# One 512 column matmul for the high and low parts of the activations, in a hybrid Conformer and gated linear attention trunk

## The chip, the cores and the metric

The kernel runs on one core of one Trainium2 chip. Its metric is the device time of one execution in microseconds. One more execution was taken by the hardware profiler: every row below comes from that one. TensorE (PE in the profile) multiplies matrices into the accumulation memory PSUM, which has 8 banks of 512 float32 columns in each of 128 partitions. VectorE is DVE, ScalarE is ACT, GpSimd is POOL, and SyncE (SP) issues the loads.

## The reference

Two layers work on 256 tokens of width 2048, in float32. Layer 0 mixes tokens with a causal Conformer convolution module, layer 1 with chunked gated linear attention (GLA). Each mixer is followed by a SwiGLU network of inner width 5632, and each half has an RMS norm ahead of it:

```
h = rms_norm(x, norm_mix_g[i]);  x = x + mixer(h)
a, g = split(rms_norm(x, norm_ffn_g[i]) @ w_gate_up[i])
x = x + (silu(a) * g) @ w_down[i]
```

At the end stands a last RMS norm. What matters here is the dense products: activations of 256 tokens by weights of 2048 (or 5632) rows.

## The kernel before

Activations lie transposed: 128 channels of one tile on the partitions, 256 tokens (T) along the columns; 16 tiles make the width of 2048. A weight matrix comes from memory in chunks of 128 x 4 x 512 float32 (1 MB), four row tiles by 512 output channels, into a ring of four buffers (`raw`). For each chunk ScalarE writes the high part `w_hi` (a copy into the type fp32r, L435), and VectorE or GpSimd writes `w_lo = raw - w_hi` (L673, L337). The activations are split in the same way, `x_hi` and `x_lo` for the normed input of a block, `h_hi` and `h_lo` for the hidden values. These four were separate SBUF tensors of 16 KB in each partition, `x_lo` right behind `x_hi`, `h_lo` right behind `h_hi`.

A product of a chunk (`chunk`, L1067) is three fp32r matmuls of 256 columns for each of its 4 x 4 pairs of row tile and output block of 128 channels, all accumulated in the same 256 columns: `w_hi` by the high part, `w_hi` by the low part, `w_lo` by the high part. Every matmul loads its 128 x 128 weights anew. A group is the chunks (4, or 3 in the last part of a SwiGLU network) that sum up 512 output channels. Two accumulators of two banks each, `slot[0]` and `slot[1]`, take groups in turn; the semaphore `acc_read[s]` says that slot s has been read and may be used again (`free_slot`). PE counts each chunk that it has done in `w_used`; the ScalarE copy of chunk c waits for chunk c - 4 in it, so the splitting runs three chunks ahead (`AHEAD`).

The dense stages, in the order in which PE runs them: the convolution's input product (`conv_product`, L1138, other tiles); its output product (`residual_product`, 16 chunks); SwiGLU of layer 0 (132 chunks); q and k (16 chunks, `group`), v (16 chunks, L1299, 512 columns, where the activations are the stationary operand and the weights move); levels of the attention; the GLA gate (16 chunks, `group`); the GLA output product (16 chunks); SwiGLU of layer 1 (132 chunks); the transposed output rows.

A SwiGLU network runs in three parts of 4, 4 and 3 pairs. In one pair, slot 0 takes the 512 channels of `a` (half 0), slot 1 those of `g` (half 1). VectorE multiplies slot 0 by the norm's factor `rstd` (L883), ScalarE takes Silu (L578), VectorE multiplies by `rstd` again (L887) and by slot 1 (L891); ScalarE writes `h_hi` (L581), VectorE `h_lo` (L894). Then four groups of the down product add to the residual stream `res` (L850, with a bias L854), which ScalarE squares for the next norm (L463) and scales into `x_hi` (L468), and VectorE sums up (L695, L698) and splits (L726). The sum over partitions for the norm is a matmul with ones into `stat` (`statistic`, L1086), issued between half 0 and half 1 of the first pair; ScalarE takes its root (L450).

All engines work through their instructions in the order of the program, each with its own stream of waits. PSUM is full: slot 0 and slot 1 in two banks each, `stat`, `pair_s0`, `pair_s1` and `misc` in one each.

## Time and profile before

| | |
|---|---|
| median of 3 runs | 2326.99 us (2325.85 to 2328.06) |
| profiled execution, its time | 2326.2 us |
| its span, first to last instruction | 2324.4 us |
| mean granted TensorE clock | 0.991 of full speed |
| PE busy | 2283.1 us, 98% |
| DVE, ACT, POOL busy | 1318.9 us, 953.7 us, 274.5 us |
| read from memory | 396.91 MB, 172 GB/s over the span |

Matmuls are pipelined. The duration of one (283 ns for 256 columns) runs over the start of the next; what a matmul costs is the distance from start to start, which the timeline shows, or the length of an unbroken stretch divided by its count.

### The profile page before, as it was taken

To read this page: it belongs to the slowest core of one execution; us is meant where nothing else is said; L and a number is where in the kernel's file an instruction comes from. 1 tells how busy PE (TensorE), PEld (TensorE's weight loads), DVE (VectorE), ACT (ScalarE), POOL (GpSimd) and SP (SyncE) were. 2 spreads that over 40 slices of the span, in tenths; PEclk is the share of its full clock that TensorE was granted. 3 is DMA by queue.
4 is the path that set the end of the run, shared out by engine and by line. 5 is a ranking of instruction groups with operands and counts; after the bars stand their busy time and mean duration, and the time that the engine had idled before them with its cause. 6 is when DMAs were issued, how large, how long until landed. Compare 5 with 4: busy or idle time off the path is not lost.

```text
span 2324.4 us, 43601 instructions
## 1 busy us (share of the span) xinstructions
PE 2283.1 (98%) x18476; PEld 2255.2 (97%) x18476; DVE 1318.9 (57%) x1204; ACT 953.7 (41%) x822; POOL 274.5 (12%) x126
## 2 busy tenths in 40 slices
PE   7999899999999999999999999999999999999998
PEld 6999799999999999999998799999999999999998
DVE  6999756545444544445666656665454445444554
ACT  6555544333333333334444344444333333333443
POOL 4988200000000000000006610000000000000000
PEclk9999899999999999999999999999999999999999
DMA  7655255555555555555454335555545555555541
GB/s 205 184 160 164 90 185 188 187 182 181 181 181 180 181 182 188 176 192 184 162 170 142 130 109 187 176 192 175 195 172 190 181 182 182 182 186 185 184 166 73
DMA packets 249951, 400.48 MB, mean 172 GB/s; under 512 B 6375, under 2 KB 72111, under 8 KB 249823
## 3 DMA queue, kind: packets, MB, share of 16 engines
q1 hardware_dynamic: 249406, 398.74, 51.1%
q8 instruction: 79, 1.29, 0.2%
q0 software_dynamic: 240, 0.23, 0.1%
q14 instruction: 18, 0.15, 0.0%
q10 hardware_dynamic: 208, 0.07, 0.0%
HBM read 396.91 MB, written 2.10 MB: 172 GB/s over the span
## 4 chain that ended last, share of the span: by engine, by line
PE 87%; issue 5%; DVE 4%; POOL 2%; ACT 1%; DMA 1%; SPq 0%; POOLq 0%; DVEq 0%; ACTq 0%
PE slot L1067 81%; DVE dec L965 1%; POOL w_lo L337 1%; PE pair_s L1284 1%; PE slot L1299 1%; PE slot L1138 1%; DMA raw<-in_conv_w_in 1%; ACT dec L620 0%; DVE dec L964 0%; PE pair_s L1127 0%; POOL y_sum L381 0%; DVE dec L971 0%; DVE dec L972 0%; PE misc L1192 0%; PE misc L1239 0%
## 5 line engine op out<-in xcount | busy, mean ns | idle before, releaser
L673 DVE TENSOR_TENSOR w_lo<-raw,w_hi 128x2048 fp32r<-128x2048 f32 x327 | 746.8, 2291 | 742.1 <-ACT w_hi L435 742.1
L435 ACT ACTIVATE w_hi<-raw 128x2048 fp32r<-128x2048 f32 x376 | 717.0, 1910 | 820.2 <-PE slot L1067 803.0
L1067 PE MATMUL slot<-x_hi,w_hi 128*128 128x256 f32 x3328 | 942.6, 283 | 0.0
L1067 PE MATMUL slot<-x_lo,w_hi 128*128 128x256 f32 x3328 | 941.8, 283 | 0.0
L1067 PE MATMUL slot<-x_hi,w_lo 128*128 128x256 f32 x3328 | 941.8, 283 | 0.0
L1067 PEld LDWEIGHTS slot<-x_hi,w_hi 128*128 128x128 f32 x3328 | 638.9, 192 | 0.4 <-issue 0.3
L1067 PEld LDWEIGHTS slot<-x_lo,w_hi 128*128 128x128 f32 x3328 | 638.9, 192 | 0.1
L1067 PEld LDWEIGHTS slot<-x_hi,w_lo 128*128 128x128 f32 x3328 | 638.9, 192 | 0.0
L1067 PE MATMUL slot<-h_hi,w_hi 128*128 128x256 f32 x1920 | 544.1, 283 | 4.4 <-DVE h_lo L836 4.4
L1067 PE MATMUL slot<-h_hi,w_lo 128*128 128x256 f32 x1920 | 544.1, 283 | 0.0
L1067 PE MATMUL slot<-h_lo,w_hi 128*128 128x256 f32 x1920 | 544.0, 283 | 0.0
L1067 PEld LDWEIGHTS slot<-h_hi,w_hi 128*128 128x128 f32 x1920 | 369.4, 192 | 4.8 <-issue 4.8
L1067 PEld LDWEIGHTS slot<-h_lo,w_hi 128*128 128x128 f32 x1920 | 369.4, 192 | 0.0
L1067 PEld LDWEIGHTS slot<-h_hi,w_lo 128*128 128x128 f32 x1920 | 369.3, 192 | 0.0
L337 POOL TENSOR_TENSOR w_lo<-raw,w_hi 128x2048 fp32r<-128x2048 f32 x49 | 233.7, 4774 | 243.5 <-ACT w_hi L435 222.7
L1138 PE MATMUL slot<-x_hi,w_hi 128*128 128x256 f32 x480 | 135.9, 283 | 2.3 <-POOL w_lo L337 2.3
L1138 PE MATMUL slot<-x_hi,w_lo 128*128 128x256 f32 x480 | 135.8, 283 | 0.0
L1138 PE MATMUL slot<-x_lo,w_hi 128*128 128x256 f32 x480 | 135.8, 283 | 0.0
L1138 PEld LDWEIGHTS slot<-x_hi,w_hi 128*128 128x128 f32 x480 | 92.0, 192 | 2.7 <-issue 1.4
L1138 PEld LDWEIGHTS slot<-x_hi,w_lo 128*128 128x128 f32 x480 | 92.0, 192 | 0.0
L1138 PEld LDWEIGHTS slot<-x_lo,w_hi 128*128 128x128 f32 x480 | 92.0, 192 | 0.0
L419 POOL DMA_DIRECT2D gate_w<-in_gla_gate_w x1 | 1.3, 1255 | 664.4 <-PE slot L1067 664.4
(225 smaller groups left out, 1467.5 us busy)
## 6 DMA issues: line engine op xcount, KB each, us to landing
raw<-in_ffn_w_gate_up SPq DMA_DIRECT2D x176, 1024.0 KB, 4.9
raw<-in_ffn_w_down SPq DMA_DIRECT2D x88, 1024.0 KB, 5.0
raw<-in_gla_w_in SPq DMA_DIRECT2D x48, 1024.0 KB, 5.1
raw<-in_conv_w_in SPq DMA_DIRECT2D x32, 1024.0 KB, 6.0
raw<-in_conv_w_out SPq DMA_DIRECT2D x16, 1024.0 KB, 5.0
raw<-in_gla_w_out SPq DMA_DIRECT2D x16, 1024.0 KB, 5.3
x_rows<-in_x SPq DMA_DIRECT2D x4, 512.0 KB, 7.1
out<-out_rows SPq DMA_DIRECT2D x4, 512.0 KB, 3.8
```

The costliest lines, as they stand in the source:

```text
L337: nc.gpsimd.tensor_tensor(w_lo[k][:, :, :], raw[k][:, :, :], w_hi[k][:, :, :].bitcast(F32), ALU.subtract).then_inc(lo_done, 1)
L419: pool.dma_start(gate_w1[:, :, :], gla_gate_w1[0].rearrange("(k p) r -> p k r", p=P)).then_inc(gate_in, 16)
L435: nc.scalar.activation(w_hi[k][:, :, :], raw[k][:, :, :], ACT.Copy).then_inc(hi_done, 1)
L673: nc.vector.tensor_tensor(w_lo[k][:, :, :], raw[k][:, :, :], w_hi[k][:, :, :].bitcast(F32), ALU.subtract).then_inc(lo_done, 1)
L965: nc.vector.tensor_tensor(d[:, :, 1, :], c[:, :, 1, :], ref, ALU.subtract).then_inc(lev_diff, 1)
L1067: ins = mm(slot[s][:, nb, :], w[k][:, kt, cols], xx[:, k0 + kt, :], start=(first and kt == 0 and i == 0 and nb % 2 == 0), stop=(last and k ...
L1138: ins = mm(slot[t][:, 2 - 2 * h, :], conv_view(w[k])[:, kt, :], xx[:, kt, :], start=(kt == 0 and j == 0), stop=(kt == KT - 1 and j == 2))
L1284: ins = mm(pr[:, (4 * a + h) * 64:(4 * a + h + 1) * 64], d, d.rearrange("p (b h r) -> p b h r", h=2, r=s)[:, :, 1, :], start=(kk == 0), st ...
L1299: ins = mm(rows_[:, a, :], xx[:, 4 * j + kt, tok], w[j][:, kt, :], start=(j == 0 and kt == 0 and i == 0), stop=(j == 3 and kt == 3 and i = ...
```

## The change

`x_hi` and `x_lo` become the two halves of one tensor `x_both` at the same addresses, `h_hi` and `h_lo` those of `h_both`. In the output products and in the SwiGLU networks `wide_chunk` takes the place of `chunk`: one matmul of 512 columns multiplies `w_hi` by the high and the low part at once into a whole bank, and a second of 256 columns multiplies `w_lo` by the high part into the first half of that bank. A group now fills four banks, 0 to 3 for s = 0 and 4 to 7 for s = 1, so that PSUM is one tensor `bank` whose parts serve as `slot`, `stat`, `pair_s` and `misc` too. Where an accumulator is read, the two halves have to be added. In the SwiGLU pairs ScalarE first copies the second half out (`part_lo`, in the place of `act`), and VectorE adds the first half to it; in the residual groups VectorE adds one half and then the other to `res`. Since banks are shared, PE has new waits: the statistic of a SwiGLU block is issued before the last chunk of half 0 and half 1 waits for its root; before the GLA output product PE waits until the last gate group has been read; and in the output rows a `free_slot(1, ...)` stands before row group 2 instead of group 3. The products of q and k, v, the gate and the convolution's input keep their matmuls.

```diff
@@ -104,11 +104,11 @@
 
         K = 1024
         res = sb("res", [P, KT, T], 0)
-        x_hi = sb("x_hi", [P, KT, T], 16 * K, F32R)
-        x_lo = sb("x_lo", [P, KT, T], 32 * K, F32R)
+        x_both = sb("x_both", [P, 2, KT, T], 16 * K, F32R)
+        x_hi, x_lo = x_both[:, 0, :, :], x_both[:, 1, :, :]
         act = sb("act", [P, KT, T], 48 * K)
-        h_hi = sb("h_hi", [P, 16, T], 64 * K, F32R)
-        h_lo = sb("h_lo", [P, 16, T], 80 * K, F32R)
+        h_both = sb("h_both", [P, 2, 16, T], 64 * K, F32R)
+        h_hi, h_lo = h_both[:, 0, :, :], h_both[:, 1, :, :]
         raw = [sb(f"raw{i}", [P, 4, GW], (96 + 8 * i) * K) for i in range(RING)]
         w_hi = [sb(f"w_hi{i}", [P, 4, GW], (128 + 8 * i) * K, F32R) for i in range(RING)]
         w_lo = [sb(f"w_lo{i}", [P, 4, GW], (160 + 8 * i) * K, F32R) for i in range(RING)]
@@ -161,10 +161,15 @@
 
         out_rows = sb("out_rows", [P, 2, D], 64 * K)
 
-        slot = [ctx.enter_context(nc.psum_tensor(f"slot{i}", [P, 4, T], F32)) for i in range(2)]
-        stat = ctx.enter_context(nc.psum_tensor("stat", [P, 2, T], F32))
-        pair_s = [ctx.enter_context(nc.psum_tensor(f"pair_s{i}", [P, 512], F32)) for i in range(2)]
-        misc = ctx.enter_context(nc.psum_tensor("misc", [P, 512], F32))
+        bank = ctx.enter_context(nc.psum_tensor("bank", [P, 8, 512], F32))
+        slot = [bank[:, 2 * i:2 * i + 2, :].rearrange("p b (h t) -> p (b h) t", t=T) for i in range(2)]
+        stat = bank[:, 4, :].rearrange("p (h t) -> p h t", t=T)
+        pair_s = [bank[:, 5 + i, :] for i in range(2)]
+        misc = bank[:, 7, :]
+
+        from_hi = [bank[:, 4 * i:4 * i + 4, 0:T] for i in range(2)]
+        from_lo = [bank[:, 4 * i:4 * i + 4, T:2 * T] for i in range(2)]
+        part_lo = [act[:, 4 * i:4 * i + 4, :] for i in range(2)]
 
         y_acc = [misc[:, :].rearrange("p (c t) -> p c t", c=2), stat]
 
...
@@ -574,10 +582,14 @@
                         hi_group_at(c0 // 4 + 2 * p)
                         if with_root:
                             root(n_root, rstd[:, :], stat[:, 0, :], 1.0 / D)
-                        scalar.wait_ge(acc_read[0], u0 // 2 + p + 1)
+                        scalar.wait_ge(w_used, c0 + 8 * p + 4)
+                        nc.scalar.activation(part_lo[0], from_lo[0], ACT.Copy).then_inc(lo_kept[0], 1)
+                        scalar.wait_ge(up_normed, 11 * l + first + p + 1)
                         nc.scalar.activation(tmp[0][:, :, :], tmp[0][:, :, :], ACT.Silu).then_inc(silu_done, 1)
                         hi_group_at(c0 // 4 + 1 + 2 * p)
-                        scalar.wait_ge(acc_read[1], u0 // 2 + p + 1)
+                        scalar.wait_ge(w_used, c0 + 8 * p + 8)
+                        nc.scalar.activation(part_lo[1], from_lo[1], ACT.Copy).then_inc(lo_kept[1], 1)
+                        scalar.wait_ge(mixed, 11 * l + first + p + 1)
                         nc.scalar.activation(h_hi[:, ds(4 * p, 4), :], tmp[1][:, :, :], ACT.Copy).then_inc(hid_hi, 1)
 
                     if pt == 0:
...
-            def residual_group(c_end, use, g, bias=None):
+            def residual_group(c_end, s, g, n_group, bias=None):
 
                 dve.wait_ge(w_used, c_end + 1)
+                to = res[:, ds(4 * g, 4), :]
                 if bias is None:
-                    nc.vector.tensor_tensor(res[:, ds(4 * g, 4), :], slot[use % 2][:, :, :], res[:, ds(4 * g, 4), :],
-                                            ALU.add).then_inc(acc_read[use % 2], 1)
-                    return
-                for b in range(4):
-                    ins = nc.vector.scalar_tensor_tensor(out=res[:, 4 * g + b, :], in0=slot[use % 2][:, b, :],
-                                                         scalar=vcol(bias, 4 * g + b), in1=res[:, 4 * g + b, :],
-                                                         op0=ALU.add, op1=ALU.add)
-                ins.then_inc(acc_read[use % 2], 1)
-
-            def residual_and_squares(c0, use0, n0, gains, chunks=4, bias=None, order=False):
+                    nc.vector.tensor_tensor(to, from_hi[s], to, ALU.add).then_inc(res_added, 1)
+                else:
+                    for b in range(4):
+                        ins = nc.vector.scalar_tensor_tensor(out=res[:, 4 * g + b, :], in0=from_hi[s][:, b, :],
+                                                             scalar=vcol(bias, 4 * g + b), in1=res[:, 4 * g + b, :],
+                                                             op0=ALU.add, op1=ALU.add)
+                    ins.then_inc(res_added, 1)
+                dve.wait_ge(res_added, n_group + 1)
+                nc.vector.tensor_tensor(to, from_lo[s], to, ALU.add).then_inc(acc_read[s], 1)
...
@@ -878,18 +892,20 @@
                         lo_group_at(c0, p, 8)
                         if with_root:
                             invert(n_root, rstd[:, :])
-                        dve.wait_ge(w_used, c0 + 8 * p + 4)
-                        dve.wait_ge(acc_read[1], u0 // 2 + p)
-                        nc.vector.tensor_tensor(tmp[0][:, :, :], slot[0][:, :, :], over(rstd[:, :], 4),
-                                                ALU.mult).then_inc(acc_read[0], 1)
+                        dve.wait_ge(lo_kept[0], 11 * l + first + p + 1)
+                        nc.vector.tensor_tensor(tmp[0][:, :, :], from_hi[0], part_lo[0], ALU.add).then_inc(acc_read[0], 1)
+                        dve.wait_ge(acc_read[0], u0 // 2 + p + 1)
+                        nc.vector.tensor_tensor(tmp[0][:, :, :], tmp[0][:, :, :], over(rstd[:, :], 4),
+                                                ALU.mult).then_inc(up_normed, 1)
                         lo_group_at(c0 + 4, p, 8)
                         dve.wait_ge(silu_done, h0 + p + 1)
                         nc.vector.tensor_tensor(tmp[0][:, :, :], tmp[0][:, :, :], over(rstd[:, :], 4),
                                                 ALU.mult).then_inc(up_scaled, 1)
+                        dve.wait_ge(lo_kept[1], 11 * l + first + p + 1)
+                        nc.vector.tensor_tensor(part_lo[1], from_hi[1], part_lo[1], ALU.add).then_inc(acc_read[1], 1)
+                        dve.wait_ge(acc_read[1], u0 // 2 + p + 1)
                         dve.wait_ge(up_scaled, 11 * l + first + p + 1)
-                        dve.wait_ge(w_used, c0 + 8 * p + 8)
-                        nc.vector.tensor_tensor(tmp[1][:, :, :], slot[1][:, :, :], tmp[0][:, :, :],
-                                                ALU.mult).then_inc(acc_read[1], 1)
+                        nc.vector.tensor_tensor(tmp[1][:, :, :], part_lo[1], tmp[0][:, :, :], ALU.mult).then_inc(mixed, 1)
                         dve.wait_ge(hid_hi, h0 + p + 1)
                         nc.vector.tensor_tensor(h_lo[:, ds(4 * p, 4), :], tmp[1][:, :, :],
                                                 h_hi[:, ds(4 * p, 4), :].bitcast(F32), ALU.subtract).then_inc(hid_ready, 1)
...
+            def wide_chunk(k, s, xx, k0, first, last, ready=None):
+
+
+                for kt in range(4):
+                    if ready is not None:
+                        pe.wait_ge(ready[0], ready[1] + kt + 1)
+                    for nb in range(4):
+                        cols = slice(nb * P, nb * P + P)
+                        to = bank[:, 4 * s + nb, :]
+                        mm(to, w_hi[k][:, kt, cols], xx[:, :, k0 + kt, :], start=(first and kt == 0), stop=False,
+                           skip_group_check=True)
+                        ins = mm(to[:, 0:T], w_lo[k][:, kt, cols], xx[:, 0, k0 + kt, :], start=False,
+                                 stop=(last and kt == 3), skip_group_check=True)
+                ins.then_inc(w_used, 1)
+
+            def wide_group(c0, k0, s, chunks, xx, ready, per_chunk=False, before_last=None):
+
+                for j in range(chunks):
+                    if before_last is not None and j == chunks - 1:
+                        before_last()
                     pe.wait_ge(lo_done, c0 + j + 1)
                     if per_chunk:
...
-                        group(c0 + 4 * s + 8 * p, 0, s, 4, x_hi, x_lo, (x_ready, x0))
+                        wide_group(c0 + 4 * s + 8 * p, 0, s, 4, x_both, (x_ready, x0), before_last=before_last)
 
                     if pt == 0:
-                        half(0, 0)
-                        statistic(stat[:, 0, :], sq_sum[:, :], sum_done, n_sum)
+                        half(0, 0, lambda: statistic(stat[:, 0, :], sq_sum[:, :], sum_done, n_sum))
+                        pe.wait_ge(root_done, n_root + 1)
                         half(0, 1)
                     with pe.Fori(1 if pt == 0 else 0, pairs) as p:
                         for s in range(2):
...
@@ -1326,8 +1365,9 @@
                 statistic(head_stat[h], head_sq[h], sum_done, 9 + h)
             for g in range(1, HEADS):
                 gate_product(g)
-            residual_product(C_GLA_OUT, U_GLA_OUT, h_hi, h_lo, (hid_ready, HID_GLA), True)
-            ffn(1, 4 * KT, 16)
+            free_slot(1, (U_R + 3) // 2 + 1)
+            residual_product(C_GLA_OUT, U_GLA_OUT, (hid_ready, HID_GLA), True)
+            ffn(1, 4 * KT, 16, 8)
 
 
             def output_rows(g, a):
...
+            free_slot(1, U_OUT // 2)
             output_rows(2, 0).then_inc(out_t, 1)
             pe.wait_ge(sum_done, 19)
             pe.wait_ge(sq_done, 20)
```

## Rows read from the trace of the kernel before

**Rows 1.** The profile's page: busy time of each engine.
```profile
PE 2283.1 (98%) x18476; PEld 2255.2 (97%) x18476; DVE 1318.9 (57%) x1204; ACT 953.7 (41%) x822; POOL 274.5 (12%) x126
```

**Rows 2.** The page: the chain that ended last, by line, as shares of the span.
```profile
PE slot L1067 81%; DVE dec L965 1%; POOL w_lo L337 1%; PE pair_s L1284 1%; PE slot L1299 1%; PE slot L1138 1%; DMA raw<-in_conv_w_in 1%; ACT dec L620 0%; DVE dec L964 0%; PE pair_s L1127 0%; POOL y_sum L381 0%; DVE dec L971 0%; DVE dec L972 0%; PE misc L1192 0%; PE misc L1239 0%
```

**Rows 3.** The waits, whole kernel: engine, line, awaited: us, times, longest.
```profile
ACT w_hi L435 <- PE slot L1067: 803.0, 238, 9.6
...
DVE w_lo L673 <- ACT w_hi L435: 742.1, 291, 5.2
...
PE slot L1067 <- DVE h_lo L836: 4.4, 1, 4.4
```

**Rows 4.** The chain in order of time: start us, us, what, count.
```profile
264.38 116.91 PE slot L1067 x960
...
381.72 760.31 PE slot L1067 x6336
...
1142.46 5.63 PE misc L1239 x48
...
1249.15 3.80 PE pair_s L1284 x32
...
1310.61 3.80 PE pair_s L1284 x32
...
1387.39 184.31 PE slot L1067 x1536
...
1572.12 737.28 PE slot L1067 x6144
```

**Rows 5.** Timeline of PE, start of the v product: start us, us, what.
```profile
1221.32 0.40 PE L1299 MATMUL slot<-w_hi,x_hi 128*128 128x512 f32 x1
...
1222.48 0.39 PE L1299 MATMUL slot<-w_hi,x_lo 128*128 128x512 f32 x1
...
1231.51 0.39 PE L1299 MATMUL slot<-w_hi,x_lo 128*128 128x512 f32 x1
...
1235.59 0.39 PE L1299 MATMUL slot<-w_hi,x_lo 128*128 128x512 f32 x1
```

**Rows 6.** Timeline of ACT and DVE, end of a SwiGLU pair in layer 1.
```profile
1635.51 1.91 ACT L435 ACTIVATE w_hi<-raw 128x2048 fp32r<-128x2048 f32 x1 [3.85 <-PE slot L1067]
1641.34 1.22 DVE L891 TENSOR_TENSOR tmp<-slot,tmp 128x1024 f32<-128x1024 f32 x1 [0.46 <-PE slot L1067]
1642.70 1.06 ACT L581 ACTIVATE h_hi<-tmp 128x1024 f32 x1 [5.28 <-DVE tmp L891]
1643.93 1.22 DVE L894 TENSOR_TENSOR h_lo<-tmp,h_hi 128x1024 f32 x1 [1.36 <-ACT h_hi L581]
1645.60 2.29 DVE L673 TENSOR_TENSOR w_lo<-raw,w_hi 128x2048 fp32r<-128x2048 f32 x1 [0.45 <-ACT w_hi L435]
```

**Rows 7.** Timeline of DVE and ACT, start of layer 1's SwiGLU.
```profile
1548.69 1.22 DVE L850 TENSOR_TENSOR res<-slot,res 128x1024 f32<-128x1024 f32 x1 [1.46 <-PE slot L1067]
1557.89 6.69 DVE L673 TENSOR_TENSOR w_lo<-raw,w_hi 128x2048 fp32r<-128x2048 f32 x3
1566.03 1.92 ACT L435 ACTIVATE w_hi<-raw 128x2048 fp32r<-128x2048 f32 x1 [3.84 <-PE slot L1067]
1567.97 1.28 ACT L450 ACT_TABLE_LOAD   x1
1572.16 0.47 ACT L450 ACTIVATE rstd<-stat,eps 128x256 f32<-128x256 f32 x1 [2.91 <-PE stat L1086]
```

**Rows 8.** Timeline of PE and DVE, from gate to GLA output product.
```profile
1456.33 0.28 PE L1067 MATMUL slot<-h_hi,w_hi 128*128 128x256 f32 x1
1456.53 1.22 DVE L1025 TENSOR_TENSOR tmp<-slot,rstd 128x1024 f32<-128x1024 f32 x1 [1.46 <-PE slot L1067]
```

**Rows 9.** Timeline of DVE and PE at the kernel's end.
```profile
2309.43 1.22 DVE L850 TENSOR_TENSOR res<-slot,res 128x1024 f32<-128x1024 f32 x1 [13.63 <-PE slot L1067]
2310.57 1.98 DVE L695 TENSOR_REDUCE sq_part<-tmp 128x256 f32<-128x1024 f32 x1
2312.58 0.43 DVE L698 TENSOR_TENSOR sq_sum<-sq_sum,sq_part 128x256 f32<-128x256 f32 x1
2313.07 0.38 PE L1351 MATMUL stat<-ones,sq_sum 128*128 128x1 f32 x2 [1.49 <-DVE sq_sum L698]
```

More of the change, by code:

```diff
@@ L218, in trunk @@
         up_scaled = sem("up_scaled")
+        lo_kept = [sem(f"lo_kept{i}") for i in range(2)]
+        up_normed = sem("up_normed")
+        mixed = sem("mixed")
+        res_added = sem("res_added")
         z1_done = sem("z1_done")
@@ L255, in trunk @@
         z_bank = [pair_s[0][:, :], pair_s[1][:, :], misc[:, :], stat[:, :, :].rearrange("p a t -> p (a t)")]
-        out_bank = [[slot[0][:, 2 * a:2 * a + 2, :].rearrange("p b t -> p (b t)") for a in range(2)],
-                    z_bank[0:2], z_bank[2:4],
-                    [slot[1][:, 2 * a:2 * a + 2, :].rearrange("p b t -> p (b t)") for a in range(2)]]
+        out_bank = [[bank[:, 0, :], bank[:, 1, :]], [bank[:, 2, :], bank[:, 3, :]],
+                    [bank[:, 7, :], bank[:, 4, :]], [bank[:, 5, :], bank[:, 6, :]]]
         head_stat = [stat[:, 0, :], misc[:, 0:T], pair_s[0][:, 0:T], pair_s[1][:, 0:T]]
@@ L870, in residual_and_squares @@
                     gain_remainders(*gains, 3)
-            residual_and_squares(C_CONV_OUT, U_CONV_OUT, 0, ("norm_ffn", 0, 2 * KT), bias="conv_b_out", order=True)
+            residual_and_squares(C_CONV_OUT, 0, 0, ("norm_ffn", 0, 2 * KT), bias="conv_b_out", order=True)
             def ffn(l, n_sq, n_root, gains):
@@ L900, in ffn @@
                         pair(p)
-                    d0, du = c0 + 8 * pairs, u0 + 2 * pairs
+                    d0 = c0 + 8 * pairs
                     if pt < 2:
@@ L905, in ffn @@
                                 lo_group_at(d0 + 4 * g, i, 8)
-                                residual_group(d0 + 4 * g + 3 + 8 * i, g, 2 * i + g)
+                                residual_group(d0 + 4 * g + 3 + 8 * i, g, 2 * i + g, 4 + 16 * l + 4 * pt + 2 * i + g)
                     else:
-                        residual_and_squares(d0, du, n_sq, gains, chunks=pairs)
+                        residual_and_squares(d0, 4 + 16 * l + 4 * pt, n_sq, gains, chunks=pairs)
             ffn(0, 4, 2, ("norm_mix", KT, 3 * KT))
@@ L1070, in chunk, with group @@
                 ins.then_inc(w_used, 1)
-            def group(c0, k0, s, chunks, x1, x2, ready, per_chunk=False):
+            def group(c0, k0, s, chunks, x1, x2, ready):
                 for j in range(chunks):
+                    pe.wait_ge(lo_done, c0 + j + 1)
+                    chunk((k0 + j) % RING, s, x1, x2, 4 * j, j == 0, j == chunks - 1, (ready[0], ready[1] + 4 * j, 1))
+            def wide_chunk(k, s, xx, k0, first, last, ready=None):
[14 more added lines that the diff above has]
+                        before_last()
                     pe.wait_ge(lo_done, c0 + j + 1)
@@ L1079, in group @@
                     else:
-                        rd = (ready[0], ready[1] + 4 * j, 1)
-                    chunk((k0 + j) % RING, s, x1, x2, 4 * j, j == 0, j == chunks - 1, rd)
+                        rd = (ready[0], ready[1] + 4 * j)
+                    wide_chunk((k0 + j) % RING, s, xx, 4 * j, j == 0, j == chunks - 1, rd)
             def statistic(to, src, ready, count):
@@ L1196, in _, with residual_product @@
             ins.then_inc(stat_done, 1)
-            def residual_product(c0, u0, x1, x2, ready, per_chunk, chunks=4):
+            def residual_product(c0, u0, ready, per_chunk, chunks=4):
                 if chunks == RING:
@@ L1203, in residual_product @@
                             free_slot(s, u0 // 2 + i)
-                            group(c0 + 4 * s + 8 * i, 0, s, 4, x1, x2, ready, per_chunk)
+                            wide_group(c0 + 4 * s + 8 * i, 0, s, 4, h_both, ready, per_chunk)
                 else:
@@ L1207, in residual_product, with ffn, half @@
                         free_slot(g % 2, (u0 + g) // 2)
[L1208 to L1210 removed]
+                        wide_group(c0 + chunks * g, c0 + chunks * g, g % 2, chunks, h_both, ready, per_chunk)
+            def ffn(l, x0, n_sum, n_root):
                 for pt, (first, pairs) in enumerate(PARTS):
                     c0, u0, h0 = C_FFN[l] + 48 * pt, U_FFN[l] + 12 * pt, HID[l] + first
[L1213 removed]
+                    def half(p, s, before_last=None):
                         free_slot(s, u0 // 2 + p)
[L1215 removed]
+                        wide_group(c0 + 4 * s + 8 * p, 0, s, 4, x_both, (x_ready, x0), before_last=before_last)
                     if pt == 0:
[L1218 to L1219 removed]
+                        half(0, 0, lambda: statistic(stat[:, 0, :], sq_sum[:, :], sum_done, n_sum))
+                        pe.wait_ge(root_done, n_root + 1)
                         half(0, 1)
@@ L1223, in ffn @@
                             half(p, s)
-                    residual_product(c0 + 8 * pairs, u0 + 2 * pairs, h_hi, h_lo, (hid_ready, h0), True, pairs)
-            residual_product(C_CONV_OUT, U_CONV_OUT, h_hi, h_lo, (x_ready, KT), False)
-            ffn(0, 2 * KT, 4)
+                    residual_product(c0 + 8 * pairs, u0 + 2 * pairs, (hid_ready, h0), True, pairs)
+            residual_product(C_CONV_OUT, U_CONV_OUT, (x_ready, KT), False)
+            ffn(0, 2 * KT, 4, 2)
             def qk_product(g):
@@ L1352, in _ @@
             ins.then_inc(stat_done, 1)
-            free_slot(1, U_OUT // 2)
             output_rows(3, 0)
```

8 lines of the change are left out of this document (3 added, 5 removed).

## The prediction, made before the changed kernel ran

> **What bounds the kernel now.** I read the page first. PE is busy 98% of the span and DVE 57%, ACT 41% [rows 1]; but pipelined matmuls always look busy, so this alone proves nothing. The chain that ended last says more: 81% of the span is L1067, the three-matmul product, with no other engine in between [rows 2]. The waits agree from the other side: ScalarE's splitting copy waits 803 us for PE, VectorE's split follows that copy, and PE's only wait at L1067 is 4.4 us, once [rows 3]. Producers wait for PE, not PE for them. Last, the chain in order of time gives the price of one matmul: 737.28 us / 6144 = 120.0 ns, and the same in the other three stretches (184.31 / 1536; 760.31 / 6336; 116.91 / 960 is 121.8, with a few slow starts at its head) [rows 4]. So what counts is PE's time from start to start, and how many starts there are.
>
> **What a wide matmul costs.** Only the v product has fp32r matmuls of 512 columns at full clock. In steady flow 18 of them take 1235.59 - 1231.51 = 4.08 us, 226.7 ns each [rows 5]. From 256 to 512 columns it goes up by 106.7 ns, 0.417 ns a column, which is one column per cycle at the 2.4 GHz level. Taken off the 120.0 ns, 256 columns leave 13.3 ns; off the 226.7 ns, 512 columns leave 13.3 ns too. So each fp32r matmul with its 128 column weight load pays columns plus 13.3 ns, whatever its width. The change keeps 768 columns for each row tile and output block but makes two starts of three: 226.7 + 120.0 = 346.7 ns for 360.0 ns. That both sizes give the same remainder is my reason to let them add up in alternation, which no row shows.
>
> **The gain.** Wide chunks are 16 (convolution output) + 132 + 16 (GLA output) + 132 = 296 of the 328 that L1067 does; times 16 pairs of row tile and block, 4736 matmuls fewer. 4736 x 13.3 ns = **63.1 us**.
>
> Bounds of that term. Worse: the first five wide matmuls after a run of short ones take 1222.48 - 1221.32 = 1.16 us, 232 ns each [rows 5], and each wide one now follows a short one. If that is the price of the switch, a pair costs 352 ns and the gain is 4736 x 8 ns = 37.9 us. Better: 256 columns with a weight tile of only 16 columns take 5.63 / 48 = 117.3 ns [rows 4], 2.7 ns less; if a load under a long matmul hides as well, the gain rises by 4736 x 2.7 ns = 12.8 us, to 75.9 us. I take the middle, since the steady wide rows and the short ones both carry full loads and leave the same 13.3 ns.
>
> A rule beside that: the Trainium skill ("TensorE: Matmul & The Clock Gate", Back-to-back issue gap) puts the gap at columns / 2.4 + 2.5 ns. By it three short matmuls would be 327.5 ns and the new two 325.0 ns, a gain of 2.5 ns or 11.8 us in all. The trace does not agree: 120.0 ns against the rule's 109.2 ns.
>
> **What the waits add.**
>
> GLA output product. PE used to go straight from the last gate group (in slot 1) to slot 0, its first matmul at 1456.33. Now group 0 needs banks 2 and 3, which are slot 1, so PE waits for VectorE's read of it, which starts at 1456.53 and takes 1.22 [rows 8]: until 1457.8, a stall of 1.45 us, with the restart 1.5 (1.4 to 1.8). VectorE is waiting for it already (its row names PE as releaser), so nothing is queued ahead of it. ScalarE's copies behind it are three chunks ahead.
>
> The end. After the last matmul the chain runs over VectorE's residual add (2309.43), the reduction (2310.57), the sum (2312.58) and PE's statistic (2313.07) [rows 9]. A second add of 1.22 us goes in between, behind a wait for the first: +1.25 us (1.14, the present distance of the two, to 1.4). ScalarE's square and gains start from the same `acc_read` and move along. The `free_slot(1)` now ahead of row group 2 clears some 2.6 us after the last matmul, before the statistic that is later than it: nothing more.
>
> SwiGLU pair. Evacuation becomes copy (ScalarE), add, multiply (VectorE). I cost it at nothing, covered by PE's next chunks. Before, `h_lo` was there 1643.93 + 1.22 - 1641.34 = 3.8 us after the group's end [rows 6]. Now 1.06 (copy, by ScalarE's row of 1024 elements) + 1.22 + 1.22 + 1.06 + 1.22 and some 0.4 of handing over = 6.2 us; the down product first needs it for the chunk at position `pairs` - 1, in the part of three pairs 2 x 5.55 = 11.1 us later. A chunk is now 16 x 346.7 ns = 5.55 us. Behind the new waits on ScalarE stands the split of the next chunk: VectorE ended it 6.5 us after the group [rows 6], now about 8.9; PE wants it after three chunks, 16.6 us. Without that cover each pair would cost 2.4 us, 53 us over 22 pairs. Both slots have a whole group of the other (22 us, 16.6 with three chunks) to be read in.
>
> Residual groups. One more VectorE add of 1.22 us each. The tightest place is the start of a SwiGLU block. The group ends about 1548.6 and VectorE comes to the first split, of chunk 3, at 1557.89, ready 2.2 later, 11.5 us after the end [rows 7]. Now it is 12.8, wanted at 3 x 5.55 = 16.6: 3.8 us to spare, nothing lost.
>
> Statistic and root. The statistic takes the same 0.42 us (between the last two stretches of [rows 4]), only earlier; its sum is formed before the `x_lo` that the last chunk needs anyway. PE then waits for the root. ScalarE starts its last split copy when the third chunk ends (1566.03), then table load and root: 1.92 + 1.28 + 0.47 = 3.7 us [rows 7]. The last chunk and the statistic cover 5.55 + 0.42 = 6.0. No stall; without the cover, 3.7 us, twice.
>
> Load. VectorE gets 2 x 22 + 32 = 76 more passes, 93 us on 1319; ScalarE 44, 47 us on 954. Against PE's 2280 neither becomes the bound. The weight stream asks 1 MB each 5.55 us for 5.76; ScalarE's copies wait for PE, not for loads [rows 3].
>
> **Sum.** -63.1 + 1.5 + 1.25 = **-60.4 us**. The profiled execution of 2326.2 us (0.8 under the median) becomes 2265.8, the median 2326.99 becomes **2266.6 us**.
>
> **Rivals.**
>
> *The switch costs.* Each wide matmul keeps 232 ns: -37.9 + 2.75 = -35.2, 2291.8 us. For it: those first five rows. Against it: the excess fades within the run though every load stays the same, so it looks like a start-up.
>
> *Only a small gain.* The remainder is not paid per start: what PE hands over or loads between starts grows with the width in this mix, and some 2.5 ns per pair stay. 4736 x 2.5 = 11.8 us, less 2.75: 2318 us. Against it stand both steady rows. This is what the skill's gap formula, in the section named above, would make of the change.
>
> *No change.* A pair takes 360 ns less just what the waits cost: 0.6 ns per pair. It needs the fixed 13.3 ns to return inside the wide one; little speaks for it.
>
> *Slower: the second piece.* The wide operand is two pieces of 256 columns 16 KB apart, where each of the present ones is a single piece. If the jump costs p ns, the change loses from p = 60.4 us / 4736 = 12.8 ns. At twice the fixed part, 26.7 ns, it is 126.5 - 60.4 = +66 us: 2393. Against it: in the attention levels, moving operands of one piece of 64 columns and of 16 pieces of 4 take the same 3.80 us for 32 [rows 4]. That is plain float32, which streams slower, so it doesn't exclude it.
>
> *Loads hide.* Gain 75.9 - 2.75: 2253.8 us.
>
> **Chances.** Forecast 0.70 (its own range 2258 to 2276); switch 0.11; small gain 0.05; loads hide 0.05; no change 0.03; slower 0.06. Range 2256 to 2294: it holds the forecast and the switch, and leaves out loads hiding, small gain, none and loss, 0.19. What a measurement can tell from no change is about 0.2%. Faster by more than that 0.91, within it 0.03, slower 0.06.
>
> **What would show it.** PE with 13740 matmuls for 18476. The last stretch of layer 1's SwiGLU (128 chunks) 710 us for 737.3; wide starts 226 to 228 ns before the short one, short 120. A new wait of PE for VectorE at the GLA output product, about 1.5 us, and none for the root, `acc_read`, `hid_ready` or `lo_done` elsewhere. From last matmul to end 1.25 us more. Wrong would be: a wide start over 230 ns throughout; PE waits at each pair; or a granted clock that falls.

## The result

The changed kernel runs in 2270.09 us (median of 4, 2267.19 to 2273.1), the kernel before in 2326.73 us (median of 4) beside it. The ratio is 0.9756 (95% interval 0.9739 to 0.9773), 56.6 us faster where 60.4 were forecast. In a second job it had 2270.0 us (5 runs) against 2325.27 us: 0.976 (0.9747 to 0.9774). The times of the first job lie in two pairs, 2267.19 and 2267.62 us, and 2272.55 and 2273.1 us. The profile read below was taken of the slowest of them, 2273.1 us, with a span of 2271.3 us; the profile of the second job has a span of 2269.5 us.

The page of the changed kernel, busy times and instructions, to be read against [rows 1]:

```profile
PE 2229.0 (98%) x13740; PEld 1992.4 (88%) x13740; DVE 1406.9 (62%) x1280; ACT 994.0 (44%) x866; POOL 274.9 (12%) x126
```

13740 matmuls, 4736 fewer. PE's busy share is unchanged at 98%, which again says nothing; but the weight loads (PEld) no longer fill the span (88% for 97%); there are 4736 fewer of them too. VectorE has 88 us more, ScalarE 40.

The lines of the changed kernel: L1103 is the wide matmul, L1105 the short one behind it, L1083 the product of three matmuls that stays in q, k and the gate, L1125 the statistic, L1290 the second product of the GLA gate, L1338 the v product, L863 and L871 the two additions to `res`, L1376 the output rows.

PE's waits, those that bear on the change (line, releaser, us in total, times, longest):

```profile
PE bank L1103 <- DVE h_both L848: 4.4, 1, 4.4
...
PE bank L1103 <- DVE tmp L1041: 1.7, 1, 1.7
...
PE bank L1376 <- DVE res L871: 0.8, 1, 0.8
```

At L1103 there are two: the 4.4 us at the convolution's output product that were there before [rows 3], and a new one, 1.7 us for VectorE's L1041, which reads the last gate group. No pair and no root appears. The 0.8 us at L1376 are the output rows behind the moved `free_slot`.

The chain in order of time, at the borders of the stages, to be read against [rows 4] (start us, us, what, count):

```profile
263.74 0.77 PE bank L1103
...
372.92 0.43 PE bank L1125 x2
1088.88 23.02 PE bank L1083 x192
...
1141.44 4.21 PE bank L1290 x16
1145.65 48.72 PE bank L1083 x384
...
1359.87 69.12 PE bank L1083 x576
1429.01 1.24 DVE tmp L1041
...
1430.67 0.47 PE bank L1103
1538.32 0.43 PE bank L1125 x2
2254.31 1.24 DVE res L863
```

The stages subtract as follows. Before, the first dense block (convolution output and SwiGLU) began at 264.38, and q and k began one group of 192 matmuls (23.04 us) ahead of their statistic at 1142.03, so at 1118.99; the gate ended where the GLA output product began, at 1456.33.

| stage | before, us | after, us | difference |
|---|---|---|---|
| up to the convolution's output product | 264.38 | 263.74 | -0.6 |
| convolution output and SwiGLU, layer 0 | 854.6 | 825.1 | -29.5 |
| q and k to the end of the gate | 337.3 | 340.1 | +2.8 |
| wait at the GLA output product | 0 | 1.7 | +1.7 |
| GLA output and SwiGLU, layer 1 | 853.1 | 823.6 | -29.5 |
| from the last add's start to the end | 15.0 | 17.0 | +2.0 |

The sum is -53.1 us, the difference of the spans. The two dense blocks give 58.9 us, 4.2 less than the forecast 63.1. The +2.8 us between q and the gate doesn't come in every execution of the changed kernel: in experiment 1 the same stage takes 337.4 us, as before.

In the dense blocks two paces are seen. The timeline of PE in the SwiGLU of layer 0:

```profile
999.97 0.39 PE L1103 MATMUL bank<-x_both,w_hi 128*128 128x512 f32 x1
1000.20 0.27 PE L1105 MATMUL bank<-x_both,w_lo 128*128 128x256 f32 x1
1000.31 0.40 PE L1103 MATMUL bank<-x_both,w_hi 128*128 128x512 f32 x1
...
1002.05 0.39 PE L1103 MATMUL bank<-x_both,w_hi 128*128 128x512 f32 x1
```

and in the GLA output product:

```profile
1450.17 0.40 PE L1103 MATMUL bank<-h_both,w_hi 128*128 128x512 f32 x1
...
1453.35 0.40 PE L1103 MATMUL bank<-h_both,w_hi 128*128 128x512 f32 x1
```

The first is 2.08 us for 6 pairs, 346.7 ns each, the forecast number. It holds over the whole last stretch: from the statistic's end (1538.75) to the last add (2254.31) 129 chunks, 2064 pairs, take 715.6 us. The second is 3.18 us for 9 pairs, 353.3 ns. The slow pace holds from 263.7 to the statistic at 372.9 and from 1430.7 to the one at 1538.3. Each of these two stretches has 19 chunks, the 16 of the output product and 3 of the SwiGLU network: 2 x 19 x 16 = 608 pairs, by 6.7 ns 4.1 us. That is nearly all of the 4.2 us that the dense blocks lack.

### The profile page after: what moved, and what is told of

The parts are those of the page before. It is cut to its first block, busy times and chain, and to the rows that moved or that the text cites. A ratio compares the mean times of both kernels' runs of the same rounds, so it can differ in the third digit from the quotient of the medians.

```text
span 2271.3 us, 34327 instructions
## 1 busy us (share of the span) xinstructions
PE 2229.0 (98%) x13740; PEld 1992.4 (88%) x13740; DVE 1406.9 (62%) x1280; ACT 994.0 (44%) x866; POOL 274.9 (12%) x126
## 3 DMA queue, kind: packets, MB, share of 16 engines
q1 hardware_dynamic: 249406, 398.74, 52.9%
## 4 chain that ended last, share of the span: by engine, by line
PE 86%; issue 5%; DVE 4%; POOL 2%; ACT 1%; DMA 0%; POOLq 0%; DVEq 0%; ACTq 0%
PE bank L1103 48%; PE bank L1105 24%; PE bank L1083 8%; DVE dec L981 1%; POOL w_lo L345 1%; PE bank L1323 1%; PE bank L1338 1%; PE bank L1177 1%; ACT dec L632 1%; DVE dec L980 0%; PE bank L1166 0%; POOL y_sum L389 0%; DVE dec L987 0%; DVE dec L988 0%; DMA vec_rows<-in_final_norm_g 0%
## 5 line engine op out<-in xcount | busy, mean ns | idle before, releaser
L1103 PE MATMUL bank<-x_both,w_hi 128*128 128x512 f32 x2816 | 977.6, 394 | 0.0
L1105 PE MATMUL bank<-x_both,w_lo 128*128 128x256 f32 x2816 | 780.4, 277 | 0.0
L1103 PE MATMUL bank<-h_both,w_hi 128*128 128x512 f32 x1920 | 671.0, 396 | 6.1 <-DVE h_both L848 4.4
L1103 PEld LDWEIGHTS bank<-x_both,w_hi 128*128 128x128 f32 x2816 | 528.0, 188 | 122.8
L1105 PE MATMUL bank<-h_both,w_lo 128*128 128x256 f32 x1920 | 534.5, 278 | 0.0
L1105 PEld LDWEIGHTS bank<-x_both,w_lo 128*128 128x128 f32 x2816 | 528.8, 188 | 0.1
L1103 PEld LDWEIGHTS bank<-h_both,w_hi 128*128 128x128 f32 x1920 | 361.0, 188 | 92.1 <-issue 6.7
L1105 PEld LDWEIGHTS bank<-h_both,w_lo 128*128 128x128 f32 x1920 | 361.8, 188 | 0.0
L1083 PE MATMUL bank<-x_both,w_hi 128*128 128x256 f32 x1024 | 187.3, 286 | 0.0
L1177 PE MATMUL bank<-x_both,w_hi 128*128 128x256 f32 x960 | 173.4, 283 | 2.7 <-POOL w_lo L345 2.7
L1083 PEld LDWEIGHTS bank<-x_both,w_hi 128*128 128x128 f32 x1024 | 161.8, 194 | 0.7 <-issue 0.7
L817 DVE SCALAR_TENSOR_TENSOR bank<-u,dw,bank 128x256 f32<-128x256 f32 x386 | 155.4, 486 | 0.0
L1177 PEld LDWEIGHTS bank<-x_both,w_hi 128*128 128x128 f32 x960 | 149.5, 192 | 3.1 <-issue 1.8
L1083 PE MATMUL bank<-x_both,w_lo 128*128 128x256 f32 x512 | 145.9, 285 | 0.0
L1177 PE MATMUL bank<-x_both,w_lo 128*128 128x256 f32 x480 | 135.8, 283 | 0.0
L1083 PEld LDWEIGHTS bank<-x_both,w_lo 128*128 128x128 f32 x512 | 99.4, 194 | 0.0
L1177 PEld LDWEIGHTS bank<-x_both,w_lo 128*128 128x128 f32 x480 | 92.0, 192 | 0.0
L1338 PE MATMUL bank<-w_hi,x_both 128*128 128x512 f32 x256 | 82.3, 396 | 0.0
```

The source lines that it names most:

```text
L817: nc.vector.scalar_tensor_tensor(out=acc, in0=u[:, t, j:j + T], scalar=w, in1=acc, op0=ALU.mult, op1=ALU.add).then_inc(tap_done, 1)
L1083: ins = mm(slot[s][:, nb, :], w[k][:, kt, cols], xx[:, k0 + kt, :], start=(first and kt == 0 and i == 0 and nb % 2 == 0), stop=(last and k ...
L1103: mm(to, w_hi[k][:, kt, cols], xx[:, :, k0 + kt, :], start=(first and kt == 0), stop=False, skip_group_check=True)
L1105: ins = mm(to[:, 0:T], w_lo[k][:, kt, cols], xx[:, 0, k0 + kt, :], start=False, stop=(last and kt == 3), skip_group_check=True)
L1177: ins = mm(slot[t][:, 2 - 2 * h, :], conv_view(w[k])[:, kt, :], xx[:, kt, :], start=(kt == 0 and j == 0), stop=(kt == KT - 1 and j == 2))
L1338: ins = mm(rows_[:, a, :], xx[:, 4 * j + kt, tok], w[j][:, kt, :], start=(j == 0 and kt == 0 and i == 0), stop=(j == 3 and kt == 3 and i = ...
```

## The experiments

**1. The changed kernel again.** No edit.

> The changed kernel as it stands, for a second profile and more times. What is open is 4 us between the forecast 2266.6 us and the median 2270.1 us. In the first profile of the changed kernel a pair of a wide and a short matmul takes 353.3 ns from the start of the convolution's output product to the first statistic, and from the start of the GLA output product to the next statistic, and 346.7 ns everywhere else; and TensorE's clock is at half for 6.8 us in the q and k stage. Theory A (pace): the 353.3 ns stretches are a property of the program, so they come again in the same two places, 640 pairs by 6.7 ns, 4.3 us. Theory B (accident): they are a chance of that one execution, as the clock may be, and are absent or elsewhere in this profile; a time near 2267 us then goes with their absence.

2270.0 us (2269.55 to 2271.23). Theory A holds: the slow pace is there again in the same two places, up to 373.87 and up to 1536.55. The 640 pairs of the expectation above are 608 by the trace: 19 chunks in each place, not 20. TensorE's clock was at half after the gate's second product here too, for 3.4 us instead of 6.8. The later stretch at half clock, among the attention's levels (the kernel before has one too, at 1326), is then shorter: 6.8 us, for 10.2 in the first profile and in the kernel before. From the start of q and k (1089.82) to the gate's end (1427.23) it is 337.4 us, as before the change.

**2. The merging undone, all else kept.**

> The changed kernel with the wide matmul cut back into two of 256 columns, high into the first half of the bank and low into the second: the banks, the additions at the eviction and all new waits stay, only the merging is undone. Theory A (a start costs 13.3 ns whatever its width): 360.0 ns per triple, and over the kernel before only the new waits, 2.75 us forecast (3.7 us by the first profile: 1.7 at the GLA output product, 2.0 at the end): 2329 to 2331 us. Rival (the layout itself helps or hurts): clearly under 2326 or over 2333 us, with PE waiting at pairs.

```
-    mm(to, w_hi[k][:, kt, cols], xx[:, :, k0 + kt, :], start=(first and kt == 0), stop=False, ...)
+    for part in range(2):
+        mm(to[:, part * T:part * T + T], w_hi[k][:, kt, cols], xx[:, part, k0 + kt, :],
+           start=(first and kt == 0 and part == 0), stop=False, ...)
```

2331.3 us (10 runs) against 2325.27: 1.0023 (1.0014 to 1.0033), 6.0 us slower than the kernel before and 61.3 slower than the changed kernel of the same job. So the merging alone gives the gain; banks, additions and waits, with the stretches at half clock around them, cost 6 us. That is more than both my forecasts of it. Its chain (in order of time) shows where the 6 us are not:

```profile
375.74 0.43 PE bank L1126 x2
1119.20 23.04 PE bank L1083 x192
...
1459.17 0.47 PE bank L1104 x2
1568.83 0.43 PE bank L1126 x2
2312.33 1.24 DVE res L863
```

From its start at 264.58 the first dense block takes 854.6 us, the second 853.2, as before to a tenth: at the pairs the additions cost nothing. The rest stands outside: 1.7 us of wait, 1.0 between q and the gate (a second stretch at half clock among the attention's levels, at 1282), 0.2 at the start, and at the end 18.3 us for 15.0. Against the profile of experiment 1 the dense blocks differ by 59.0 us; the other 2.1 us of the spans' difference lie between q and the gate and at the end, where the clock differs.

**3. A filler matmul.**

> The changed kernel with one more float32 matmul with ones, of 256 columns, into the unused bank 4 before the last chunk of the first group of the convolution's and of the GLA's output product (its result is not used; those two products are written out instead of looped). In the first profile the pace goes from 353.3 to 346.7 ns right behind such a matmul, the statistic. Theory A (the float32 matmul lets the weight loads run ahead again): the pace changes at the filler, 12 chunks plus 4 earlier than now; 16 of 20 chunks at each place have 346.7 ns less 0.43 us for the filler: about 3.4 us in the first place and in the second together less 0.9, 2.5 us, and the profile shows 346.7 ns behind each filler. Rival (the pace hangs on something else that ends at the same time, such as the hidden operand or the stage's waits): 353.3 ns stays behind the filler until the statistic, and the time is 0.9 us over that of the unchanged changed kernel.

```
+    def fill():
+        mm(stat[:, 0, :], ones[:, :], ones[:, :].unsqueeze(1).broadcast_to([P, 2, P]), start=True, stop=True)
...
+    wide_group(..., before_last=fill if i == 0 and s == 0 else None)
```

2268.68 us (2267.45 to 2269.77), 1.3 us under the changed kernel of the same job; the interval of its ratio (0.9741 to 0.9768) overlaps that one's, so the time alone doesn't decide. The trace does. (Written out instead of looped, the product also starts 0.4 us sooner behind its wait: 1.3 us of wait for 1.7.) The chain around the second filler:

```profile
1426.48 0.50 PE bank L1103
1443.71 0.43 PE bank L1240 x2
1532.89 0.43 PE bank L1125 x2
```

From the first wide matmul to the filler, three chunks take 1443.71 - 1426.48 = 17.23 us, a pair 359 ns with the slow head of the first chunk. From the filler's end (1444.14) to the statistic 16 chunks take 88.75 us: 346.7 ns a pair. The pace changed at the filler, and in the first block in the same way. From the first wide matmul to the statistic the two stretches take 1.3 and 1.2 us less than in the changed kernel, as forecast. Theory A holds in that; what kind of matmul does it, experiment 4 tells.

**4. An ordinary fp32r matmul as filler.**

> As the filler kernel, but the one added matmul is an ordinary fp32r one of 256 columns (hidden activations by themselves, result not used) in place of the float32 one. Theory A1 (any extra start without a wide partner shifts the phase): the pace goes from 353.3 to 346.7 ns behind it. Theory A2 (it takes the float32 matmul, which streams twice 213 ns and gives the weight loads time to run ahead): 353.3 ns stays until the statistic.

```
-    mm(stat[:, 0, :], ones[:, :], ones[:, :].unsqueeze(1).broadcast_to([P, 2, P]), start=True, stop=True)
+    mm(stat[:, 0, :], h_both[:, 0, 0, 0:P], h_both[:, 0, 1, :], start=True, stop=True)
```

2271.18 us, one run; the time decides nothing. PE's timeline around the second filler (L1240):

```profile
1444.72 0.40 PE L1103 MATMUL bank<-h_both,w_hi 128*128 128x512 f32 x1
...
1445.78 0.40 PE L1103 MATMUL bank<-h_both,w_hi 128*128 128x512 f32 x1
1446.02 0.28 PE L1105 MATMUL bank<-h_both,w_lo 128*128 128x256 f32 x1
1446.14 0.28 PE L1240 MATMUL bank<-h_both 128*128 128x256 f32 x1
...
1446.62 0.39 PE L1103 MATMUL bank<-h_both,w_hi 128*128 128x512 f32 x1
...
1448.70 0.39 PE L1103 MATMUL bank<-h_both,w_hi 128*128 128x512 f32 x1
```

Ahead of it three pairs take 1.06 us, 353 ns each; behind it six pairs take 2.08 us, 346.7. So theory A2 falls: one more short start, 0.12 us, was enough in this one place. In this execution the first block ran at 346.7 ns already ahead of its filler, after 6.8 us at half clock around its head where the changed kernel had 3.4. The slow pace is thus a state that the stream of matmuls can have from its start and keeps until something breaks the alternation. A wait ahead of it is not enough, since this first block stands behind a wait of 4.4 us, and not needed, as experiment 8 shows. What sets the pace at the start, and why it is stable, is open.

**5. One piece for two.**

> The changed kernel with the wide matmul reading 512 adjacent columns, the high parts of this and the preceding tile, instead of two pieces 16 KB apart (the low part of the activations is left out of the products; the first tile of each group stays as it is). Theory A (a jump costs nothing): 346.7 ns per pair in the long stretches and a time like that of the changed kernel, 2267 to 2273 us. Rival (the second piece costs part of the 232 ns of a wide start): the pair falls under 346 ns; each ns less is 4.4 us.

```
-    xx[:, :, k0 + kt, :]
+    (xx[:, 0, k0 + kt - 1:k0 + kt + 1, :] if k0 + kt else xx[:, :, 0, :])
```

2271.85 us (2270.05 to 2272.85), and PE's timeline in the long stretch:

```profile
999.67 0.39 PE L1103 MATMUL bank<-x_both,w_hi 128*128 128x512 f32 x1
...
1001.06 0.39 PE L1103 MATMUL bank<-x_both,w_hi 128*128 128x512 f32 x1
```

Four pairs in 1.39 us, 347 ns, and the two dense blocks take 824.9 and 823.6 us, for 825.1 and 823.6 in the changed kernel. The jump of 16 KB costs nothing; theory A holds.

**6. A small weight load under the long matmul.**

> The changed kernel with the short matmul of each pair loading 16 weight columns instead of 128 (so of the low weights' product only 16 of 128 output channels are computed). Theory A (the 13.3 ns of a start does not depend on the load, which lies under the long matmul): 346.7 ns per pair in the long stretches. Rival, from the 117.3 ns of the 16 column rows before: 344.0 ns per pair, 12 us less in all.

```
-    ins = mm(to[:, 0:T], w_lo[k][:, kt, cols], xx[:, 0, k0 + kt, :], ...)
+    ins = mm(to[0:16, 0:T], w_lo[k][:, kt, nb * P:nb * P + 16], xx[:, 0, k0 + kt, :], ...)
```

In PE's timeline of the long stretch nine pairs take 1002.79 - 999.67 = 3.12 us: 346.7 ns. At the good pace the size of the load under the long matmul is no part of the price, and the rival of 344 ns falls. The one time taken, 2267.92 us, shows no gain of 12 us either.

In the slow stretches the load may matter. The chain from the GLA output product to its statistic, after the same wait of 1.7 us as in the changed kernel:

```profile
1426.30 0.47 PE bank L1103
1531.94 0.43 PE bank L1125 x2
```

It takes 105.64 us for 107.65 in the changed kernel: with the small load this stretch ran at 346.7 ns without any filler. In the first block its pace was 350.0 ns a pair, for 353.3. No other profile shows either, but this is one execution, and the first block's pace varies without any small load too (experiment 4). That the size of the load bears on which pace the stream falls into is possible, not shown.

**7. Four wide, then four short.**

> The changed kernel with the order changed inside a row tile: first the four wide matmuls of the four output blocks, then the four short ones, the same work. Theory A (each start costs 13.3 ns whatever stands ahead of it): 4 x 346.7 = 1386.7 ns per row tile in the long stretches, as now. Theory C (a wide matmul behind a short one costs some 5 ns more, a short one behind a wide one some 5 ns less, as the single starts of 230 to 233 and 112 to 119 ns look): the sum stays too, but the starts inside read 226.7 and 120. The 353.3 ns phase ahead of the statistics: if it belongs to the alternation, it is gone here, 4.3 us less than the changed kernel; if it belongs to the start after a wait, it stays.

```
     for nb in range(4):
         ...
+        mm(bank[:, 4 * s + nb, :], w_hi[k][:, kt, cols], xx[:, :, k0 + kt, :], ...)
+    for nb in range(4):
         ...
+        ins = mm(bank[:, 4 * s + nb, 0:T], w_lo[k][:, kt, cols], xx[:, 0, k0 + kt, :], ...)
```

2286.57 us, ratio 0.9831 (0.9816 to 0.9846): 16.5 us slower than the changed kernel's 2270 of the other job, with the same matmuls. Neither theory had that. Its timeline in the long stretch:

```profile
1000.67 1.09 PE L1102 MATMUL bank<-x_both,w_hi 128*128 128x512 f32 x4
1001.59 0.64 PE L1106 MATMUL bank<-x_both,w_lo 128*128 128x256 f32 x4
1002.07 1.09 PE L1102 MATMUL bank<-x_both,w_hi 128*128 128x512 f32 x4
```

A row tile of 4 pairs takes 1.40 us, 350 ns a pair. Four wide take 0.92 us of it (230 each, where steady wide ones took 226.7 [rows 5]), four short 0.48 (120 each). The dense blocks measure it better: in its chain they begin at 263.52 and 1435.44 and end at 1096.25 and 2266.88, 7.6 and 7.8 us over the changed kernel's; the second gives 350.9 ns a pair over the whole block, its statistic taken off. So 13.3 ns a start whatever stands ahead of it is not a rule. It holds in a steady stream of one width and for strict alternation at its good pace.

**8. Four remedies together.**

> Four remedies for what the changed kernel loses against the forecast: the float32 filler before the second chunk of the two output products (19 of 20 chunks at 346.7 ns: 4.05 us less 0.86); the last gate group in banks 5 and 6, so that PE need not wait for its eviction at the GLA output product (1.6 us); the products of the gate's second weight split in two around a chunk, so that the clock does not fall there (1.4 to 2.8 us); seven unused fp32r matmuls while PE waits for the last sum, to keep the clock up at the end (0.8 us). Sum 7 to 9 us: 2261 to 2263 us where the changed kernel has 2270. Rival for each: the pace, the wait or the half clock shows up again elsewhere, and the time stays over 2267 us.

```
+                                       before_last=fill if i == 0 and s == 0 else None, before_at=1)
...
+                group(C_R + 4 * g, 0, 2 if g == 3 else g % 2, 4, x_hi, x_lo, (x_ready, 3 * KT))
...
+            z_products((0, 1))
+            for j in range(4):
+                if j == 1:
+                    z_products((2, 3))
...
+                chunk(j, 0, x_hi, x_lo, 4 * j, j == 0, j == 3, (x_ready, 3 * KT + 4 * j, 1))
...
+            for j in range(7):
+                mm(bank[:, 5, :], w_hi[0][:, 0, 0:P], x_both[:, :, j, :], start=True, stop=True)
```

`before_at=1` puts the filler ahead of the second chunk; slot 2 is banks 5 and 6.

2265.35 us (2264.68 to 2265.89), ratio 0.9739 (0.9726 to 0.9752): some 4.7 us under the changed kernel's 2270 in the jobs before. The intervals of the two ratios just touch (0.9752 here, 0.9747 in experiment 1), so the size is rough. It is not the forecast 7 to 9. Its chain from the gate's second product on:

```profile
1139.61 1.92 PE bank L1301 x8
...
1149.40 40.51 PE bank L1084 x336
...
1356.60 69.11 PE bank L1084 x576
1431.36 0.43 PE bank L1241 x2
...
2247.62 1.23 DVE res L864
```

The wait is gone: from the gate's end at 1425.71 to the filler is one chunk, 5.65 us. PE's timeline there:

```profile
1425.42 0.28 PE L1084 MATMUL bank<-x_both,w_lo 128*128 128x256 f32 x1
1425.54 0.40 PE L1104 MATMUL bank<-h_both,w_hi 128*128 128x512 f32 x1
...
1431.20 0.59 PE L1241 MATMUL bank<-ones 128*128 128x256 f32 x2
```

The first wide matmul starts 0.12 us behind the last of the gate, without a wait, and yet its chunk runs at the slow pace: 16 pairs in 5.66 us, some 353 ns each. Behind the filler 18 chunks take 99.84 us, 346.7 ns a pair. In the first block the pace was 346.7 ns ahead of the filler already, as in experiment 4, again after 6.8 us at half clock; that block took 0.6 us less than in the changed kernel, the second 1.7.

The stage from the start of q and k to the gate's end is 1425.71 - 1087.05 = 338.7 us. The split product took 1139.61 to 1189.91, 50.3 us for 52.9 in the first profile, but TensorE's clock now fell to half once more among the attention's levels. That is 1.4 us less than the first profile's 340.1 and 1.3 more than the 337.4 of experiments 1, 3 and 6, where the product wasn't split: a gain of this remedy is not shown. The end is 16.5 us with a granted clock of 0.81, for 17.0 with 0.68. But the same end without the seven matmuls took from 16.7 to 18.3 us in the eight other profiles since the change, so from one execution no more can be said than that they gain something between 0.2 and 1.8 us.

## Why the prediction was right, point by point

**The bound.** Right: PE sets the time before and after, and 59.0 us in the dense blocks hang on the number of its starts alone (experiment 2).

**The gain term, 63.1 us.** Right in mechanism, 4.2 us too large. I took 346.7 ns for all 4736 pairs; 4128 have it, 608 have 353.3. The step that failed is "I take the middle, since the steady wide rows and the short ones both carry full loads and leave the same 13.3 ns". Equal remainders in two steady streams didn't prove that they add up in a mixed one. They do in alternation at its good pace, but experiment 7 shows the same matmuls at some 350 ns in another order. The single starts are of neither steady stream: 0.23 us for the wide and 0.11 to 0.12 for the short, which is the rival's 232 ns for the wide, repaid by the short one. The prediction called "a wide start over 230 ns throughout" a sign of being wrong, with 226 to 228 and 120 expected. That sign came, while the pair cost what was forecast: it is the pair that counts, and that the two deviations cancel was not reasoned out but lucky.

**Loads hide.** No: the fastest pace seen is 346.7 ns, with 16 weight columns too. The 117.3 ns of [rows 4] don't carry over. What the small load may do is keep the slow pace away or soften it (experiment 6).

**GLA output product, 1.5 us.** Measured 1.7, at the place and by the releaser that the prediction names; experiment 8 removes it.

**The end, 1.25 us.** Measured 2.0 in the first profile, and 1.7 to 3.3 over the profiles with this end (16.7 to 18.3 us, for 15.0 in the one profile of before). The second add itself was costed right. VectorE at the end of the changed kernel:

```profile
2254.31 1.23 DVE L863 TENSOR_TENSOR res<-bank,res 128x1024 f32<-128x1024 f32 x1 [11.73 <-PE bank L1105]
2255.57 1.23 DVE L871 TENSOR_TENSOR res<-bank,res 128x1024 f32<-128x1024 f32 x1
```

What was missed is the clock. PE idles longer, and the granted clock of the last 17.0 us is 0.68 where the last 15.0 us had 0.74 before; in the profile with 18.3 us it is 0.63. The windows from the last add to the end, before and after (us, busy and count of PE, PEld, DVE, ACT, POOL; granted clock, DMA share, GB/s):

```profile
2309.43:2324.40 14.97, 6.10 (x52) 5.46 (x50) 6.44 (x8) 6.62 (x11) 0.00 (x0) 0.74 0.35 140
```

```profile
2254.31:2271.30 16.99, 8.25 (x52) 7.37 (x50) 7.65 (x9) 6.84 (x11) 0.00 (x0) 0.68 0.31 123
```

The same 52 matmuls are busy 8.25 us for 6.10.

**The pair, the residual groups, statistic and root, at nothing.** Right. ScalarE and VectorE at the end of a pair in layer 1, to be read against [rows 6]:

```profile
1566.52 1.03 ACT L591 ACTIVATE act<-bank 128x1024 f32<-128x1024 f32 x1 [3.57 <-PE bank L1105]
1570.10 1.06 ACT L593 ACTIVATE h_both<-tmp 128x1024 fp32r<-128x1024 f32 x1 [2.55 <-DVE tmp L908]
1571.06 3.71 ACT L443 ACTIVATE w_hi<-raw 128x2048 fp32r<-128x2048 f32 x2
```

```profile
1571.19 1.23 DVE L910 TENSOR_TENSOR h_both<-tmp,h_both 128x1024 fp32r<-128x1024 f32 x1 [1.12 <-ACT h_both L593]
```

From the start of the copy to the low part it is 1571.19 + 1.23 - 1566.52 = 5.9 us, forecast 6.2. ScalarE's next split then runs as a double at 1571.06: it was late and catches up, while PE waits for nobody.

**Not foreseen.** TensorE's clock fell to half after the gate's second product (L1290, 16 matmuls with 16 rows of weights). The window of the changed kernel:

```profile
1144.40:1151.20 6.80, 6.80 (x30) 6.06 (x29) 3.81 (x5) 4.57 (x3) 0.00 (x0) 0.50 0.18 43
```

The product and the half of q and k behind it take 52.9 us (1141.44 to 1194.37) for 49.9 before; in experiment 1, with 3.4 us at half clock, 51.4. There the later stretch at half clock is shorter by as much, and the whole stage takes no longer than before; with 6.8 us, in three of the six, it takes 2.7 us more. The prediction named "a granted clock that falls" as a sign of being wrong; by this it had a small part in the time. All six profiles of kernels with alternating pairs and an unsplit product have it, for 3.4 or 6.8 us; the kernel before, the narrow one and the grouped one don't, though they have the same product. It goes with the alternating order in these nine profiles; how the one could bring the other is open.

**The number.** By the medians the gain is 3.8 us under the forecast 60.4. The first profile, the slowest execution, misses 7.3 us: 4.2 of pace, 2.8 between q and the gate (clock), 0.2 and 0.75 of wait and end, less 0.6 ahead of the dense blocks. The changed kernel's times lie up to 5.9 us apart (2267.19 to 2273.1), so part of the median's closeness to the forecast is the draw of the executions.

**Rivals.** The switch as the rival priced it (37.9 us), the small gain by the formula of the Trainium skill (11.8 us), no change, and the second piece are all excluded, the last by experiment 5.

Of the rule of the Trainium skill that the prediction weighed ("TensorE: Matmul & The Clock Gate", Back-to-back issue gap), which that section itself gives for an isolated matmul: the changed kernel's pairs at 346.7 ns disagree with its 325.0 as the short matmuls did with its 109.2.

## What to carry to other kernels

Where PE sets the time, take the price of a start from two widths in the trace (here 120.0 and 226.7 ns, 13.3 ns beyond the columns) and count starts, not columns; merge matmuls that share their stationary operand, and pay with additions on engines that have room. Then measure the pace in the real order, since the same matmuls grouped otherwise cost 16.5 us more. A new step ahead of an idle stretch can cost more than its length: the addition at the end took 1.25 us, and the end grew by 1.7 us or more.

## What the runs showed of the hardware that was not expected

A stream of alternating 512 and 256 column fp32r matmuls has more than one stable pace: 346.7 ns a pair, and 353.3 ns, which it has from its start, behind a wait of PE (the changed kernel) or straight behind 256 column matmuls (experiment 8), and keeps over 19 chunks. One more short matmul of 0.12 us (seen once), or a float32 one of 0.43 (seen in both places of experiment 3), switched it to the good one. With a small weight load in every pair it was 350.0 ns in one place and 346.7 in the other. The state can't be read from busy shares or from single durations; only start to start over several pairs shows it.

In the three profiles where the stretch at half clock after the gate's second product lasted 3.4 us, the one among the attention's levels lasted 6.8 us, the two together as long as the single one of the kernel before, 10.2. Where it lasted 6.8 us, the later one kept its 10.2.
